# Two transformer blocks on one core: the first slot of w_in taken in plain float32, and expert 0's last unit of weights loaded beside the ring

## The chip, the cores and the metric

The kernel runs on one NeuronCore of one Trainium2 chip. It is one program on that core's engines: TensorE (PE), VectorE (DVE), ScalarE (ACT), GpSimd (POOL) and SyncE (SP), which here only issues transfers. The metric is the time of one execution on the device in microseconds; less is better.

## The reference, cut to what matters

256 tokens of width 1024 pass two blocks. The first block is a conditioned transformer layer (modulation from `c @ w_ada`, norm, attention of two kinds, an MLP with squared ReLU). The second is a mixer (a linear recurrence and a differential attention, gated) followed by 16 experts. The parts that the change touches are the first projection and the experts:

```python
sh1, sc1, g1, sh2, sc2, g2 = jnp.split(c_act @ w_ada + b_ada, 6)
h = rmsnorm(x, norm_gains[0]) * (1.0 + sc1) + sh1
proj = h @ w_in                                   # (256, 1024) @ (1024, 2304)
...
aff = softmax(h @ w_router)                       # (256, 16)
g, idx = top_k(aff.T, 32)                         # each expert takes 32 tokens
xe = h[idx]                                       # (16, 32, 1024)
hid = silu(xe @ w_gate) * (xe @ w_up)             # w_gate, w_up: (16, 1024, 2048)
ye = (hid @ w_down) * g                           # w_down: (16, 2048, 1024)
out = rms_norm(x + zeros.at[idx].add(ye))
```

Everything is float32. The experts' weights are 16 x 3 x 8 MB, 403 MB in all, read once.

## The kernel before, in words

**The prelude.** All weights ahead of the experts come in 99 slots of 1 MB ([128, 2048] float32), numbered by `g`: 8 of w_ada (`G_ADA0`), 9 of w_in (`G_WIN`), 16 of w_ada, 4 of w_out, 32 of the MLP, 14 and 8 of the second w_in (`G_MIX2`, `G_GATES2`), 4 + 4 of the last projections. SP issues them in that order into a ring of 6 slots; a load waits until the slot six places earlier has been used or split. The large products run in three passes: ACT rounds a slot to fp32r (`round_slot`, L353), DVE or POOL subtracts to get the rest (`residue_slot`, L361), the activations are handled likewise (`round_tile`, `residue_tile`), and PE multiplies rounded x rounded, rounded x rest and rest x rounded (`product`, L491 to L493). The split slots have two buffers (`wR`), so `round_slot(g)` waits until PE is done with the split slot two places earlier. Slots listed in `RAW` skip all that: `raw_channels` (L532) multiplies them in plain float32, a tile of 128 tokens at a time.

**The start.** PE multiplies the 8 slots of w_ada as they arrive (`ada`, L564), turns the rows of gains and biases into columns and the modulation row into columns (`turn`, L485). DVE and ACT write the normed and modulated hidden state `hT` (`place`, L1000 and L1591), round and split it, and then the first two slots of w_in. ACT issues 14 small transfers in `late_loads()` (L1536 to L1550) behind those two slots and ahead of the third. From w_in's fourth slot comes the attention bias: DVE writes a row, POOL stores it and reads it back in 16 transfers (L1870), copies a part, and DVE waits for the copy (`bias_copied`, ahead of L1091) before the attention.

**The experts.** An expert has 6 units of 4 MB: two of w_gate, two of w_up, two of w_down, numbered `u` from 0 to 95. They go through 5 buffers (`expert_ring`, buffer `u % 5`), the memory that the prelude's ring and split buffers leave. Units 0 to 4 are issued as the prelude frees that memory; unit `u` from 5 on waits for `pairs_used`, which PE raises twice per unit when it has multiplied a half. Units of gate and up come as one transfer, each partition reading 32 KB in a row; units of down as two transfers of 2 MB with 16 KB in a row each (`halved`), as does unit 5. PE gathers the tokens of four experts (L906), multiplies gate and up with four tiles of 32 columns side by side (L931), turns the hidden values (L485), multiplies down (L956) and scatters (L964).

## Time and profile before

| | us |
|---|---|
| median of 3 runs | 1537.79 |
| lowest and highest | 1537.52, 1540.73 |
| the profiled execution, its own time | 1543.38 |
| its span in the profile | 1541.0 |

| engine | busy us | share |
|---|---|---|
| PE, multiplying | 1134.6 | 74% |
| DVE | 404.3 | 26% |
| ACT | 317.6 | 21% |
| POOL | 54.9 | 4% |

The profile cuts the span into 40 slices of 38.5 us. The first 16 or so hold the prelude, the rest are the experts. In the chain of work that ended last 52% of the span are transfers and 41% PE. A busy PE need not be at its peak; the trace gives the clock that PE was granted, at 1.00 for 2.4 GHz and 0.50 for 1.2 GHz.

### The profile page before, as it was taken

The numbers are of one execution on the slowest core, as the hardware profiler recorded it, in microseconds if no ns is written. First come the engines' busy times: TensorE is split into PE (matmuls) and PEld (weight loads), VectorE is DVE, ScalarE is ACT, GpSimd is POOL, SyncE is SP. The second block draws the span as 40 slices with busy tenths as digits, with TensorE's granted clock in tenths as the row PEclk, the third lists the DMA queues.
The fourth block names the chain that finished last, engine by engine and source line by source line (L and its number), as shares of the span: only waits on it lengthen the run. The fifth ranks groups of instructions, "written<-read, shape, count | busy, mean of one in ns | idle before, by whom it ended". The sixth has DMA issues, their size and how long they took to land.

```text
span 1541.0 us, 17000 instructions
## 1 busy us (share of the span) xinstructions
PE 1134.6 (74%) x7468; PEld 667.3 (43%) x7468; DVE 404.3 (26%) x731; ACT 317.6 (21%) x543; POOL 54.9 (4%) x50
## 2 busy tenths in 40 slices
PE   3999999998999779965657656657656567565555
PEld 1976898987999778411113111113111113111111
DVE  2447664655758664200000000000000000000001
ACT  3346453444644544000000000000000000000001
POOL 0020000000024300000000000000000000000000
PEclk8898999999999889978778877878788868778777
DMA  9879356552753247899999999999999999999996
GB/s 366 284 279 375 109 198 191 185 189 87 222 167 110 83 164 323 344 428 430 433 427 430 433 426 432 431 426 432 431 427 433 429 429 430 430 430 429 430 432 268
DMA packets 91507, 516.43 MB, mean 335 GB/s; under 512 B 6847, under 2 KB 63658, under 8 KB 71978
## 3 DMA queue, kind: packets, MB, share of 16 engines
q1 hardware_dynamic: 86400, 508.57, 81.3%
q10 hardware_dynamic: 4106, 4.57, 0.9%
q0 software_dynamic: 928, 2.20, 0.5%
q8 instruction: 59, 0.97, 0.3%
q14 instruction: 14, 0.11, 0.0%
HBM read 514.12 MB, written 1.07 MB: 334 GB/s over the span
## 4 chain that ended last, share of the span: by engine, by line
DMA 52%; PE 41%; DVE 4%; ACT 2%; issue 1%; ACTq 0%; SPq 0%; DVEq 0%
DMA expert_ring<-in_w_up_e 19%; DMA expert_ring<-in_w_gate_e 17%; DMA expert_ring<-in_w_down_e 15%; PE PS L491 9%; PE PS L492 9%; PE PS L493 9%; PE PS L931 6%; PE PS L485 2%; DMA ring<-in_w_ada 1%; PE PS L956 1%; PE PS L564 1%; PE PS L906 1%; PE PS L532 1%; DVE wR L361 1%; PE PS L526 0%
## 5 line engine op out<-in xcount | busy, mean ns | idle before, releaser
L931 PE MATMUL PS<-expert_ring,xeT 128*32 128x512 f32 x2048 | 350.0, 847 | 239.2 <-DMA expert_ring<-in_w_up_e 121.3
L931 PEld LDWEIGHTS PS<-expert_ring,xeT 128*32 128x32 f32 x2048 | 81.4, 148 | 506.4 <-issue 238.7
L1501 DVE TENSOR_TENSOR expert_rows<-expert_rows,PS 128x512 f32<-128x512 f32 x16 | 11.0, 687 | 819.4 <-PE PS L931 819.4
L491 PE MATMUL PS<-hR,wR 128*128 128x256 f32 x648 | 187.4, 289 | 16.3 <-DVE wR L361 16.3
L956 PE MATMUL PS<-expert_ring,expert_rows 128*32 128x512 f32 x1024 | 141.0, 687 | 73.0 <-DMA expert_ring<-in_w_down_e 64.2
L353 ACT ACTIVATE wR<-ring 128x1024 fp32r<-128x1024 f32 (+2 forms) x146 | 146.3, 1051 | 217.1 <-PE PS L493 217.1
L492 PE MATMUL PS<-hR,wR 128*128 128x256 f32 x648 | 185.9, 287 | 0.0
L493 PE MATMUL PS<-hR,wR 128*128 128x256 f32 x648 | 185.7, 287 | 0.0
L361 DVE TENSOR_TENSOR wR<-ring,wR 128x1024 fp32r<-128x1024 f32 x130 | 153.2, 1221 | 106.4 <-ACT wR L353 106.3
L491 PEld LDWEIGHTS PS<-hR,wR 128*128 128x128 f32 x648 | 127.1, 196 | 18.4 <-issue 18.3
L492 PEld LDWEIGHTS PS<-hR,wR 128*128 128x128 f32 x648 | 127.2, 196 | 0.0
L493 PEld LDWEIGHTS PS<-hR,wR 128*128 128x128 f32 x648 | 126.9, 196 | 0.0
L956 PEld LDWEIGHTS PS<-expert_ring,expert_rows 128*32 128x32 f32 x1024 | 30.5, 118 | 167.0 <-DMA expert_ring<-in_w_down_e 99.6
L491 PE MATMUL PS<-wR,hR 128*128 128x256 f32 (+1 forms) x272 | 78.5, 288 | 3.1 <-DVE wR L361 1.6
L1833 ACT ACTIVATE expert_rows<-PS 128x512 f32<-128x512 f32 x16 | 9.6, 597 | 339.8 <-PE PS L931 339.8
L492 PE MATMUL PS<-wR,hR 128*128 128x256 f32 (+1 forms) x272 | 78.0, 287 | 0.0
L493 PE MATMUL PS<-wR,hR 128*128 128x256 f32 (+1 forms) x272 | 78.0, 287 | 0.0
L1838 ACT ACTIVATE selx<-PS 128x256 f32<-128x256 f32 x16 | 6.1, 383 | 342.9 <-PE PS L485 342.9
L491 PEld LDWEIGHTS PS<-wR,hR 128*128 128x128 f32 x272 | 53.5, 197 | 5.9 <-DVE hR L1436 2.3
L492 PEld LDWEIGHTS PS<-wR,hR 128*128 128x128 f32 x272 | 53.5, 197 | 0.0
L493 PEld LDWEIGHTS PS<-wR,hR 128*128 128x128 f32 x272 | 53.4, 196 | 0.0
L1840 ACT ACTIVATE expert_rows<-PS 128x512 f32<-128x512 f32 x16 | 9.6, 597 | 208.3 <-PE PS L956 208.3
(256 smaller groups left out, 1074.9 us busy)
## 6 DMA issues: line engine op xcount, KB each, us to landing
expert_ring<-in_w_gate_e SPq DMA_DIRECT2D x32, 4096.0 KB, 42.9
expert_ring<-in_w_up_e SPq DMA_DIRECT2D x32, 4096.0 KB, 43.6
expert_ring<-in_w_down_e SPq DMA_DIRECT2D x64, 2048.0 KB, 43.6
ring<-in_w SPq DMA_DIRECT2D x32, 1024.0 KB, 5.5
ring<-in_w_in SPq DMA_DIRECT2D x31, 1024.0 KB, 5.8
ring<-in_w_ada SPq DMA_DIRECT2D x24, 1024.0 KB, 9.9
ring<-in_w_out SPq DMA_DIRECT2D x8, 1024.0 KB, 8.8
arena<-bias_scratch POOLq DMA_DIRECT2D x16, 128.0 KB, 5.8
```

What stands on the lines that cost most here:

```text
L353: nc.scalar.activation(halves(g, 0)[:, piece], slot(g)[:, piece], ACT.Copy).then_inc(slot_rounded, 1)
L361: by.tensor_tensor(halves(g, 1)[:, piece], slot(g)[:, piece], halves(g, 0)[:, piece], ALU.subtract)\
L485: return nc.tensor.transpose(out_, in_, ident[0:n, 0:n])
L491: nc.tensor.matmul(o, first[0], second[0], start=start, stop=False, skip_group_check=onto)
L492: nc.tensor.matmul(o, first[0], second[1], start=False, stop=False, skip_group_check=onto)
L493: return nc.tensor.matmul(o, first[1], second[0], start=False, stop=stop, skip_group_check=onto)
L532: mm = nc.tensor.matmul(PS[:, bank, m * S + t * P:m * S + (t + 1) * P], k8(g)[:, k, m * P:(m + 1) * P], hT[:, k, t * P:(t + 1) * P], start ...
L564: mm = nc.tensor.matmul(PS[32 * j:32 * j + 32, bank, :], crep[:, k, :], slot(g)[:, 512 * j:512 * (j + 1)], start=(k == 0), stop=(k == 7), ...
L906: mm = nc.tensor.matmul(o, work[:, t, k::KD], sel[t][:, GROUP * group:GROUP * (group + 1), :] .rearrange("p e c -> p (e c)"), start=(t == ...
L931: mm = nc.tensor.matmul(PS[32 * j:32 * j + 32, kind // 2, :], xeT[:, e // GROUP % 2, k, own], w[:, 512 * j:512 * (j + 1)], start=(k == 0), ...
L956: mm = nc.tensor.matmul(PS[32 * at:32 * at + 32, 3, :], hidT[:, c, q, :], w[:, c, 512 * half:512 * (half + 1)], start=(q == 0 and c < 2), ...
L1501: V.tensor_tensor(hid[:, :], silu[:, :], PS[:, 1, :], ALU.mult).then_inc(hid_set, 1)
```

## The change

There are five edits. (1) w_in's first slot joins `RAW`: no rounding and splitting of it; PE multiplies it per token tile as soon as that tile of `hT` is placed, and ACT places both tiles before it rounds them. (2) PE gets 30 float32 products of the identity with itself (`turned_awake`) between the slots of w_ada and behind the turned modulation row, and turns the gains' rows behind the sixth w_ada slot, not behind the eighth. (3) Expert 0's last unit (`APART`, u = 5) leaves the ring and lies in four other places: 2 MB in a new tensor `ahead`, 1 MB in `ybuf`, and half a MB each in `xeT`'s second half and in `const`. The ring now takes 95 units, counted by `fill_of` and `unit_of`. (4) w_down is laid out in two pieces of rows per expert, not four, so a partition reads 32 KB in a row and a down unit is one transfer; only unit 6 and the last are still halved. For that the hidden values must come in another order, so gate's and up's moving operand is read as runs of 4 floats with 4 left out between them. (5) To make room, the scratch for POOL's transfers is set to 1024 bytes, `selx` moves into `const`, and a square's throwaway output goes to `work`.

```diff
 BUFFERS = 5
+APART = 5
-RAW = (G_MLP, G_MIX2)
+RAW = (G_WIN, G_MLP, G_MIX2)
+        ahead = sb("ahead", [P, 2 * SLOT])
-        selx = sb("selx", [P, S])
+        selx = nc.alloc_sbuf_tensor_at("selx", [P, S], F32, offset=const_at + 4 * C_DIST)
+        sixth = [ahead[:, c * D:(c + 1) * D] for c in range(4)] + [ahead_y[:, 0:D], ahead_y[:, D:2 * D], ahead_x, ahead_c]
+        def fill_of(u):
+            return u - (u > APART)
+        def unit_of(n):
+            return n + (n >= APART)
         def halved(u):
-            return u % UNITS_EACH >= 4 or u == BUFFERS
+            return u in (APART + 1, EXPERTS * UNITS_EACH - 1)
...
         def _(sp):
+            down = A["w_down_e_2"][0].rearrange("e (q p c) n -> e q p (c n)", q=2, p=P)
             for g, (dst, src) in enumerate(loads):
+                if g == G_GATES2 + 4:
+                    sp.dma_start(ahead[:, :], down[0, 1][:, 0:4 * D]).then_inc(ahead_loaded, 16)
...
-            down = A["w_down_e_2"][0].rearrange("e (q p c) n -> e q p (c n)", q=4, p=P)
             for u in range(EXPERTS * UNITS_EACH):
-                e, kind, b = u // UNITS_EACH, u % UNITS_EACH, u % BUFFERS
+                e, kind, n = u // UNITS_EACH, u % UNITS_EACH, fill_of(u)
+                b = n % BUFFERS
...
                 if u == 1:
+                    sp.wait_ge(act_split, 2 * TBRANCH + 2)
+                    sp.dma_start(ahead_y, down[0, 1][:, 4 * D:6 * D]).then_inc(ahead_loaded, 16)
                     sp.wait_ge(mixed, 2)
...
+                if u == APART:
+                    sp.wait_ge(logit16, 1)
+                    sp.dma_start(ahead_x, down[0, 1][:, 6 * D:7 * D]).then_inc(ahead_x_loaded, 16)
+                    sp.wait_ge(rank_cols, 1)
+                    sp.dma_start(ahead_c, down[0, 1][:, 7 * D:8 * D]).then_inc(ahead_c_loaded, 16)
+                    continue
+                if n >= BUFFERS:
+                    sp.wait_ge(pairs_used, 2 * unit_of(n - BUFFERS) + (1 if halved(u) else 2))
...
+            def turned_awake(times):
+                for _ in range(times):
+                    nc.tensor.matmul(PS[:, 1, 0:P], ident, ident, start=True, stop=True)
...
+                if k == 5:
+                    pe.wait_ge(rows_in, 16 * 5)
+                    pe.wait_ge(rows_in_pool, 16 * 4)
+                    turn(PS[:, 0, 0:A_ROWS], rowsA[:, :], A_ROWS)
+                    turn(PS[:, 0, A_ROWS:A_ROWS + B_ROWS], rowsB[:, :], B_ROWS).then_inc(cols_turned, 1)
+                if k >= 3:
+                    turned_awake(5 if k < 7 else 2)
             pe.wait_ge(modrow_set, 1)
             turn_mod(0, 3)
+            turned_awake(8)
+            for t in range(NT):
+                pe.wait_ge(placed[0], 2 * T1 + t + 1)
+                pe.wait_ge(placed[1], 2 * T1 + t + 1)
+                if t == 0:
+                    arrived(pe, G_WIN)
+                mm = raw_channels(G_WIN, 0, t)
+            mm.then_inc(slots_used, 1)
             pe.wait_ge(act_split, 2 * T1 + 2)
...
-                        w = expert_ring[:, FILL[u % BUFFERS], r * SLOT:(r + 1) * SLOT]
+                        w = expert_ring[:, FILL[fill_of(u) % BUFFERS], r * SLOT:(r + 1) * SLOT]\
+                            .rearrange("p (q n h c) -> p q h n c", q=2, n=P, h=2)
                         for j in range(4):
                             mm = nc.tensor.matmul(PS[32 * j:32 * j + 32, kind // 2, :], xeT[:, e // GROUP % 2, k, own],
-                                                  w[:, 512 * j:512 * (j + 1)], start=(k == 0), stop=(k == KD - 1),
+                                                  w[:, j // 2, j % 2, :, :], start=(k == 0), stop=(k == KD - 1),
...
-            for g in range(G_WIN, G_WIN + 2):
-                residue_slot(dve, V, g)
+            residue_slot(dve, V, G_WIN + 1)
...
-            place(T1, 4, hT, lambda k: fold[:, 0, k:k + 1], lambda k: shift1[:, k:k + 1])
-            for g in range(G_WIN, G_WIN + 2):
-                round_slot(act, g)
+            place(T1, 4, hT, lambda k: fold[:, 0, k:k + 1], lambda k: shift1[:, k:k + 1], split=False)
+            for t in range(NT):
+                round_tile(T1, hT, t)
+            round_slot(act, G_WIN + 1)
             late_loads()
...
-    nc = _bacc.Bacc("TRN2", target_bir_lowering=False, num_devices=1)
+    nc = _bacc.Bacc("TRN2", target_bir_lowering=False, num_devices=1, dynamic_dma_scratch_size=1024)
```

Line numbers in the changed file differ: `turn` is L511 there, `product` L517 to L519, `ada` L595, `raw_channels` L563, `turned_awake` L557, `round_slot` L359.

This is PE's program before, from the last three slots of w_ada to the first slot of w_in (`ring<-` here is w_ada, `hR,wR` the split hidden state and weights; [waits ...] are the semaphores ahead of an instruction):

```order
L564 MATMUL PS<-ring,crep 32x512 [waits loaded1]
L564 MATMUL PS<-ring,crep 32x512 x3
L485 MATMUL PS<-const,arena 128x112 [waits rows_in_pool,rows_in]
L485 MATMUL PS<-const,arena 128x69
L485 MATMUL PS<-const,arena 128x128 [waits modrow_set]
L485 MATMUL PS<-const,arena 128x128 x3
L491 MATMUL PS<-hR,wR 128x256 [waits slot_split_dve,act_split]
```

And the same place in the changed program (L557 with `const` alone are the added products):

```order
L595 MATMUL PS<-ring,crep 32x512 [waits loaded1]
L595 MATMUL PS<-ring,crep 32x512 x3
L557 MATMUL PS<-const 128x128 x2
L511 MATMUL PS<-const,arena 128x128 [waits modrow_set]
L511 MATMUL PS<-const,arena 128x128 x3
L557 MATMUL PS<-const 128x128 x8
L563 MATMUL PS<-hT,ring 128x128 [waits loaded2,placed_act,placed_dve]
L563 MATMUL PS<-hT,ring 128x128 x15
L563 MATMUL PS<-hT,ring 128x128 [waits placed_act,placed_dve]
L563 MATMUL PS<-hT,ring 128x128 x15
L517 MATMUL PS<-hR,wR 128x256 [waits slot_split_dve,act_split]
```

What PE does first behind the turned row no longer waits for a split, and the first split product is now that of w_in's second slot.

ACT's program around the small transfers before (`hT` placed and rounded per tile, then two slots rounded, then the transfers, of which the first and last are shown, then the third slot):

```order
L1600 ACTIVATE hR<-hT 128x8x128 [waits placed_act,placed_dve]
L353 ACTIVATE wR<-ring 128x1024 [waits loaded2]
L353 ACTIVATE wR<-ring 128x1024
L353 ACTIVATE wR<-ring 128x1024 [waits loaded3]
L353 ACTIVATE wR<-ring 128x1024
L1536 DMA relb<-in_rel_bias 32x16
...
L1550 DMA arena<-in_norm_gains 128x1024
L353 ACTIVATE wR<-ring 128x1024 [waits slots_used,loaded4]
```

And in the changed program:

```order
L1651 ACTIVATE hR<-hT 128x8x128 [waits placed_act,placed_dve] x2
L359 ACTIVATE wR<-ring 128x1024 [waits loaded3]
L359 ACTIVATE wR<-ring 128x1024
L1587 DMA relb<-in_rel_bias 32x16
...
L1601 DMA arena<-in_norm_gains 128x1024
L359 ACTIVATE wR<-ring 128x1024 [waits loaded4]
```

The third slot's rounding has lost its wait for PE (`slots_used`) but still stands behind the 14 transfers.

SP's program at the experts' start, before:

```order
L465 DMA expert_ring<-in_w_gate_e 128x8192 [waits normed]
L465 DMA expert_ring<-in_w_gate_e 128x8192 [waits mixed]
L465 DMA expert_ring<-in_w_up_e 128x8192 [waits slot_split_dve]
L465 DMA expert_ring<-in_w_up_e 128x8192 [waits slots_used]
L470 DMA expert_ring<-in_w_down_e 128x4096 x2
L470 DMA expert_ring<-in_w_down_e 128x4096 [waits pairs_used] x2
L465 DMA expert_ring<-in_w_gate_e 128x8192 [waits pairs_used] x2
```

And in the changed program:

```order
L491 DMA expert_ring<-in_w_gate_e 128x8192 [waits normed]
L475 DMA ybuf<-in_w_down_e 128x2048 [waits act_split]
L491 DMA expert_ring<-in_w_gate_e 128x8192 [waits mixed]
L491 DMA expert_ring<-in_w_up_e 128x8192 [waits slot_split_dve]
L491 DMA expert_ring<-in_w_up_e 128x8192 [waits slots_used]
L491 DMA expert_ring<-in_w_down_e 128x8192
L483 DMA xeT<-in_w_down_e 128x1024 [waits logit16]
L485 DMA const<-in_w_down_e 128x1024 [waits rank_cols]
L497 DMA expert_ring<-in_w_gate_e 128x4096 [waits pairs_used] x2
L491 DMA expert_ring<-in_w_gate_e 128x8192 [waits pairs_used]
```

The first transfer that waits for PE to free a buffer is now expert 1's first gate unit; expert 0's second down unit is issued in pieces ahead of it.

## Rows read from the trace of the kernel before

**Rows 1.** The page: GB/s moved in each of 40 slices of 38.5 us.

```profile
GB/s 366 284 279 375 109 198 191 185 189 87 222 167 110 83 164 323 344 428 430 433 427 430 433 426 432 431 426 432 431 427 433 429 429 430 430 430 429 430 432 268
```

**Rows 2.** Stretches: length, busy us by engine, then PE's clock, DMA share, GB/s.

```profile
40.70:46.40 5.70, 5.64 (x26) 5.67 (x27) 2.18 (x2) 0.17 (x1) 0.00 (x0) 0.50 1.07 363
...
626.00:632.00 6.00, 6.00 (x34) 5.16 (x36) 1.72 (x3) 0.00 (x0) 0.00 (x0) 0.94 0.14 60
...
651.00:1529.00 878.00, 542.11 (x3206) 153.12 (x3202) 30.29 (x64) 23.66 (x45) 0.00 (x0) 0.80 1.00 428
```

**Rows 3.** PE in order of time, experts: start us, length us, instruction, [idle before <-releaser].

```profile
695.05 1.92 PE L956 MATMUL PS<-expert_ring,expert_rows 128*32 128x512 f32 x16 [0.48 <-DMA expert_ring<-in_w_down_e]
...
704.84 3.35 PE L956 MATMUL PS<-expert_ring,expert_rows 128*32 128x512 f32 x16 [2.97 <-DMA expert_ring<-in_w_down_e]
...
714.55 5.34 PE L931 MATMUL PS<-expert_ring,xeT 128*32 128x512 f32 x32 [3.59 <-DMA expert_ring<-in_w_gate_e]
...
734.01 6.25 PE L931 MATMUL PS<-expert_ring,xeT 128*32 128x512 f32 x32 [3.72 <-DMA expert_ring<-in_w_up_e]
```

**Rows 4.** SP's transfers in order of time at the experts' start.

```profile
606.27 28.63 SPq L470 DMA_DIRECT2D expert_ring<-in_w_down_e  x4
638.00 3.76 SPq L465 DMA_DIRECT2D expert_ring<-in_w_gate_e  x2
```

**Rows 5.** PE in order of time from the ranks' transposes to the first units.

```profile
622.15 0.29 PE L485 MATMUL PS<-const,top_rows 16*128 16x16 f32 x2 [1.06 <-DVE top_rows L1464]
...
630.87 13.94 PE L931 MATMUL PS<-expert_ring,xeT 128*32 128x512 f32 x128
```

**Rows 6.** The chain that ended last: start us, us, what.

```profile
369.93 3.57 PE PS L532 x32
...
623.02 7.92 PE PS L906 x32
...
1528.57 3.26 PE PS L956 x16
```

**Rows 7.** PE in order of time at the start, and behind one later gap.

```profile
17.71 1.06 PE L564 MATMUL PS<-ring,crep 128*32 128x512 f32 x8
...
26.47 1.94 PE L564 MATMUL PS<-ring,crep 128*32 128x512 f32 x8 [1.48 <-DMA ring<-in_w_ada]
...
30.07 1.11 PE L485 MATMUL PS<-const,arena 128*128 128x128 f32 x4 [1.17 <-DVE arena L1045]
...
509.16 1.11 PE L485 MATMUL PS<-const,arena 128*128 128x128 f32 x4 [5.02 <-DVE arena L1353]
```

**Rows 8.** The clock behind that gap.

```profile
511.00:513.00 2.00, 2.00 (x11) 2.00 (x11) 1.90 (x5) 0.10 (x1) 0.00 (x0) 0.50 0.98 332
```

**Rows 9.** DVE and ACT in order of time, w_in's first three slots (ACTq: ACT issues transfers).

```profile
31.84 2.64 DVE L1000 TENSOR_SCALAR hT<-PS,fold,modcol 128x128 f32<-128x128 f32 x8
...
34.44 1.49 ACT L1591 ACTIVATE hT<-PS,modcol,fold 128x128 f32<-128x128 f32 x4
...
36.16 0.32 ACTq L1536 DMA_DIRECT2D relb<-in_rel_bias  x1
...
47.87 0.46 ACTq L1550 DMA_DIRECT2D arena<-in_norm_gains  x1
...
49.34 2.01 ACT L353 ACTIVATE wR<-ring 128x1024 fp32r<-128x1024 f32 x2 [8.47 <-PE PS L493]
...
50.50 2.36 DVE L361 TENSOR_TENSOR wR<-ring,wR 128x1024 fp32r<-128x1024 f32 x2 [7.62 <-ACT wR L353]
...
55.10 2.01 ACT L353 ACTIVATE wR<-ring 128x1024 fp32r<-128x1024 f32 x2 [3.75 <-PE PS L493]
```

**Rows 10.** POOL reads the attention bias back; DVE's first instruction behind that wait.

```profile
76.78 8.49 POOL L1870 DMA_DIRECT2D arena<-bias_scratch  x16 [4.45 <-DMA bias_scratch<-arena]
92.21 1.89 POOL L1873 COPY arena<-arena 128x2048 f32<-128x2048 f32 x1 [6.94 <-DMA arena<-bias_scratch]
...
100.16 0.16 DVE L1091 TENSOR_SCALAR sinkneg<-sinkbc 128x8 f32<-128x8 f32 x1
```

More of the change, by code:

```diff
@@ L947, in _ @@
                 pe.wait_ge(hidT_set, e + 1)
[L948 to L953 removed]
+                for q in range(2):
+                    u = UNITS_EACH * e + 4 + q
+                    w = expert_ring[:, FILL[fill_of(u) % BUFFERS], :]
+                    w = sixth if u == APART else [w[:, c * D:(c + 1) * D] for c in range(8)]
+                    for c in range(8):
+                        if u == APART:
+                            if c % 4 == 0:
+                                pe.wait_ge(ahead_loaded, 32)
+                            if c >= 6:
+                                pe.wait_ge((ahead_x_loaded, ahead_c_loaded)[c - 6], 16)
+                        elif c % 4 == 0:
+                            unit_arrived(u, c // 4)
                         for half in range(2):
                             at = 2 * half + c % 2
[L956 to L959 removed]
+                            mm = nc.tensor.matmul(PS[32 * at:32 * at + 32, 3, :], hidT[:, c % 4, 2 * q + c // 4, :],
+                                                  w[c][:, 512 * half:512 * (half + 1)], start=(q == 0 and c < 2),
+                                                  stop=(q == 1 and c >= 6), tile_position=(0, 32 * at))
+                        if c % 4 == 3:
+                            mm.then_inc(pairs_used, 1)
                 pe.wait_ge(selx_ready, e + 1)
```

48 lines of the change are left out of this document (19 added, 29 removed).

## The prediction

> **What bounds the kernel now.** I read the page's slices first. In [rows 1] the traffic is uneven in the first seventeen slices and then stands at 426 to 433 GB/s up to the last one, and the stretch from 651 to 1529 us has a DMA share of 1.00 while PE's clock is 0.80 [rows 2]. So there are two regimes. In the experts transfers set the pace: in PE's order of time each product of a unit begins when its unit has landed, with 3 to 4 us of idle PE ahead of it [rows 3], and the chain ends with the last down half, 3.26 us of PE from 1528.57 us [rows 6]. Only fewer bytes in that stream, a better rate, or an earlier start of it shorten it. The start is set by the prelude, where PE and the split pipeline set the pace, because the transfer of unit 5 waits for PE to free half of unit 0. Between the two is a hole: from 626 to 632 us only 60 GB/s are moved [rows 2], since units 3 and 4 are through and unit 5 may not start before PE, which began at 630.87 us, has done half a unit [rows 5].
>
> **Edit 3, the sixth unit.** Before, the stream behind the hole carries units 5 to 95, 91 of them; now 6 to 95, 90. Unit 6 waits for the same half of unit 0 as unit 5 did. A down unit takes the stream 704.84 - 695.05 = 9.79 us [rows 3]: two halves landed one after the other. That is the gain, if unit 5's 4 MB lie in time when nobody needs the queue. 2 MB are issued with the gates' slots, where the slices show 83 to 167 GB/s [rows 1], against 430 possible; they push the next slot's load back by 2.1/0.43 = 4.9 us, and a slot is loaded six slots ahead, two of which the split takes, so more than 20 us of cover remain. 1 MB is issued right behind unit 0, in a wait of SP for `mixed`. The last two half MB are issued at `logit16` and at the ranks' transposes, 622.15 us [rows 5], and queue behind units 3 and 4: those were issued at 606.27 us [rows 4] and end at about 606.3 + 2 x 9.75 = 625.8 us, so the last piece lands at about 625.8 + 1.05/0.43 = 628.2 us, ahead of 632.6 us, when the stream restarts (630.87 plus half of 13.94/4 us [rows 5]). SP's new waits have only unit 6's issue queued behind them, which waits longer anyway. Cost nothing, gain **9.8 us**. Were the cover gone (all 4 MB behind 632 us), the gain would be 0.
>
> **Edit 4, longer runs.** In one and the same stream three units of gate and up land in 734.01 - 704.84 = 29.17 us, 9.72 us each, and the down unit before them took 9.79 [rows 3]. The two kinds differ in the length of the run (32 against 16 KB) and the number of transfers (one against two). With both made equal I take 0.07 us for each of 30 down units (all but unit 5, counted above, and the last): **2.1 us**. Bounds: 0, and 3 us with 0.1 us each.
>
> The price of this edit is the strided moving operand of gate and up. The trace has no strided moving operand. The nearest row is the gather L906, whose stationary operand takes one float in eight: its 32 records took 7.92 us where the 32 of the raw product L532, of the same size, took 3.57 us [rows 6], a factor of 2.2. Below nothing it can't go. At 2.2 a unit at full clock takes 3.48 x 2.2 = 7.7 us in place of 3.48, still less than the 9.72 us in which the next one lands, so it is paid once: half a unit ahead of the stream's restart, 2.1 us. I take 0, being nearer to whole runs of four than to single floats, and keep 2.1 us for the range. The Trainium skill (SBUF — State Buffer, the note on SBUF cachelines) says that accesses in one 16-byte line run at full rate and each new line costs; four floats in a row use whole lines, so by that rule this read costs nothing and the gather's eightfold step does; by the rule the sum is as I give it, by the gather's factor 2.1 us worse.
>
> **Edits 1 and 2, the start.** I follow the moment at which PE starts w_in's third slot; from there each slot is PE's as before. Before, it is 55.10 us: ACT's row there was released by PE's last product of the second slot, and the third follows at once [rows 9].
> - The last w_ada slot took 1.94 us at half clock, earlier ones 1.06 us [rows 7]. With the added products (0.22 us each by L532, 16 products in 3.57 us [rows 6]) PE hardly stands still, so I let the clock stay up: the slot ends at about 28.1 us, not 28.41. The gains' rows are already turned and copied, which takes some 0.6 us out of the way to the modulation row's turn, and that takes 0.6 in place of 1.11 us [rows 7]. So the placing starts at about 30.2 us in place of 31.84 [rows 9]: 1.6 us earlier.
> - PE starts the raw product of tile 0 at 30.2 + 1.6 = 31.8 us and works 2 x 3.6 us [rows 6], to 39.1 us. Meanwhile ACT rounds both tiles and the second slot, DVE follows; by the durations of about 1.0 and 1.2 us a piece (2.01 and 2.36 us for two [rows 9]) that is done at about 39.2 us. PE does the second slot at full clock in 48 x 0.12 = 5.76 us (55.10 - 49.34 [rows 9]), to **45.0 us**.
> - The third slot's rounding no longer waits for PE, but ACT has its transfers ahead of it. They ran from 36.16 to 48.33 us, 12.2 us, starting as soon as the second tile was placed, at 34.44 + 1.49 = 35.93 us [rows 9]. Now both tiles are placed by 30.2 + 3.0 = 33.2 us; the transfers end at about 33.4 + 12.2 = 45.6 us. From ACT's start to DVE's end the split takes 50.50 + 2.36 - 49.34 = 3.5 us [rows 9], so PE gets the third slot at **49.1 us**. This is 6.0 us earlier, with a new wait of 4.1 us in it. Before, that stretch of ACT was covered by PE's slow first slot.
> - A gap of this size costs clock: behind one of 5.02 us [rows 7] the clock was 0.50 [rows 8], and at 0.50, 26 products took 5.64 us [rows 2] that take 3.1 us at full clock, 2.5 us lost. I take 2.1 us. Net **3.9 us**.
>
> Bounds for this part: nothing, if the clock is lost longer or the attention waits for something else; and 55.10 - 45.0 = 10.1 us, if the transfers do not hold ACT up.
>
> **Edit 5.** POOL's smaller scratch could slow its 16 transfers of the bias. They are issued in 8.49 us, the last lands 6.94 us later, the copy ends at 94.10 us, and DVE comes to that wait at 100.16 us [rows 10]. All of it hangs on w_in's fourth slot and moves with it, so 6.1 us of cover remain. No row of before shows POOL waiting for room. I take 0. The moved `selx` and `work` change no instruction's size: 0.
>
> **Sum**, against the profiled execution: 1543.4 - 9.8 - 2.1 - 3.9 = 1527.6 us. The median of the runs lies 5.6 us below the profiled time, so the forecast is **1522.0 us**.
>
> **Rivals.**
> - *A, ACT's transfers don't hold the third slot up* (they are shorter when fewer other transfers run, or ACT gets to the rounding between them). For it: that 12.2 us were never on the path, so nothing shows what they really need. Against it: they stand ahead in ACT's order, and 14 of them at the 0.32 to 0.46 us of the first and the last [rows 9] are still some 5.5 us. Then the start gives 10.1 us and no clock is lost: 1537.8 - 9.8 - 2.1 - 10.1 = 1515.8 us.
> - *B, the start gives nothing, the stream gives its part:* clock lost for a whole slot behind the new gap, or the strided read at 2.2, or both; 1537.8 - 11.9 = 1525.9 us, to 1528 with the 2.1 us.
> - *C, slower: POOL's transfers run one behind the other.* In before the 16 overlap: 8.49 + 6.94 = 15.4 us in all. With room for one at a time each takes its issue of 0.53 us and some 6 us to land, 16 x 6.5 = 104 us, 89 us more; less 6.1 of cover and 15.8 of gain it is 67 us slower, 1605 us. It decides when the bias comes more than 6.1 + 15.8 = 21.9 us later, which takes two or fewer in flight (16/2 x 6.5 = 52 us against 15.4). For it: the edit cuts exactly what these transfers use. Against it: no row. No run here shows it yet. Seven in flight at some 6 us each end 3 to 4 us later than now, which the 6.1 us cover.
> - *D, the sixth unit saves nothing* because its pieces collide with what needs the queue; 1537.8 - 6.0 = 1531.8 us. Against it stand the hole and the low slices.
>
> **How the numbers follow.** Forecast (1518 to 1525): 0.68. A: 0.14. B: 0.10. C: 0.04. D: 0.03; a strided read beyond 3 times, at which PE would bound the experts and the time rise above before: 0.01. The range from 1514 to 1527.5 leaves out C, D and a part of A and B. A difference of 0.2% (3 us) is about what a measurement of this kernel can tell from none. Faster: 0.68 + 0.14 + 0.10 + 0.03 = 0.95, less 0.02 for what I have not thought of: 0.93. Same 0.02, slower 0.05.
>
> **What would show it.** Right: in the stretch of the experts transfers fill everything from about 627 - 4 us on with no second hole; the number of units behind it is 90; a down unit lands in 9.72 us; the w_in stage has an idle PE of about 4 us between second and third slot, released by DVE, behind ACT's transfers, and the clock at 0.50 behind it; gate and up take 3.5 us per unit at full clock. Wrong: a wait of DVE for POOL's copy ahead of the attention; gate and up units of 7 us; the first products at 0.50 although the warmers ran; idle transfers behind 632 us because PE frees buffers too late.

## The result

The changed kernel takes 1528.65 us, the median of six runs (1526.48 to 1532.55). Beside it the kernel before took 1538.72 us (six runs, 1537.52 to 1543.81). The ratio is 0.9935, with a 95% interval from 0.9919 to 0.9951, so the change saves about 10 us (7.5 to 12.5). A second measurement gave 1528.48 us and a ratio of 0.9933 (0.9920 to 0.9947). The forecast was 1522.0 us with a range of 1514.0 to 1527.5: the direction is right, the size is not, and the time lies 1.2 us outside the range. Of 15.8 us that the sum promised, about 10 came.

The profiled execution of the changed kernel took 1527.02 us, with a span of 1524.7 us. I read it in the order of the prediction.

**The stream.** The slices of the changed kernel (GB/s, against [rows 1]) and three stretches (columns as in [rows 2]):

```profile
GB/s 366 293 282 376 136 177 194 192 192 69 221 230 119 84 193 303 371 438 428 429 435 428 434 432 429 433 430 432 429 431 432 430 435 426 434 432 426 437 428 264
```

```profile
46.00:52.00 6.00, 2.30 (x11) 2.30 (x11) 4.72 (x5) 4.38 (x5) 0.00 (x0) 0.76 1.17 332
624.00:629.00 5.00, 5.00 (x35) 3.23 (x39) 2.11 (x5) 0.00 (x0) 0.00 (x0) 1.00 0.26 106
...
646.00:1512.00 866.00, 517.61 (x3210) 154.98 (x3198) 30.28 (x64) 23.66 (x45) 0.00 (x0) 0.82 1.00 429
```

The hole ahead of the first units is still there, and behind it nothing pauses. In PE's order of time the first units, the two down units of the second expert with the up unit ahead and the gate unit behind, and the last down half, against [rows 3, 5, 6] (a float32 product shows as two records, so x32 is 16 products):

```profile
626.54 13.94 PE L976 MATMUL PS<-expert_ring,xeT 128*32 128x512 f32 x128
...
670.94 4.99 PE L976 MATMUL PS<-expert_ring,xeT 128*32 128x512 f32 x32 [6.08 <-DMA expert_ring<-in_w_up_e]
680.74 5.21 PE L1007 MATMUL PS<-expert_ring,expert_rows 128*32 128x512 f32 x32 [3.02 <-DMA expert_ring<-in_w_down_e]
690.50 5.34 PE L1007 MATMUL PS<-expert_ring,expert_rows 128*32 128x512 f32 x32 [4.55 <-DMA expert_ring<-in_w_down_e]
...
700.21 3.64 PE L976 MATMUL PS<-expert_ring,xeT 128*32 128x512 f32 x32 [1.58 <-DMA expert_ring<-in_w_gate_e]
...
1512.14 2.46 PE L1007 MATMUL PS<-expert_ring,expert_rows 128*32 128x512 f32 x16 [2.59 <-DMA expert_ring<-in_w_down_e]
1515.40 3.78 PE L1016 MATMUL PS<-expert_rows,selx 64*128 64x512 f32 x8 [0.79 <-ACT expert_rows L1892]
```

The first four units take 13.94 us, to the hundredth what they took with whole rows [rows 5]: the strided read costs nothing. A row that waited for a transfer begins when it has landed, so the two down units here took 680.74 - 670.94 = 9.80 and 690.50 - 680.74 = 9.76 us, and the gate unit behind them 9.71. Over the whole trace the first down unit of an expert takes 9.80 us and the second 9.62 (medians), 19.43 together; in the kernel before the two take 19.6 together. So the mean is 9.71, as forecast, but it comes from the second of the two. From the first unit to the last down half pass 1512.14 - 626.54 = 885.60 us, where it was 1528.57 - 630.87 = 897.70 [rows 5, 6]: 12.1 us less, forecast were 11.9. The last row is for later: the scatter L1016 takes 3.78 us.

SP's transfers, against [rows 4]:

```profile
601.92 0.43 SPq L491 DMA_DIRECT2D expert_ring<-in_w_down_e  x1
609.31 0.33 SPq L483 DMA_DIRECT2D xeT<-in_w_down_e  x1
618.14 0.33 SPq L485 DMA_DIRECT2D const<-in_w_down_e  x1
628.52 2.04 SPq L497 DMA_DIRECT2D expert_ring<-in_w_gate_e  x2
```

The last piece of the sixth unit is issued 10 us before the stream restarts and lands 9.0 us later, at 627.1 us; none of it is behind 628.5 us.

**The start.** PE (against [rows 7]), ACT and DVE ([rows 9]):

```profile
27.61 1.07 PE L595 MATMUL PS<-ring,crep 128*32 128x512 f32 x8 [0.81 <-DMA ring<-in_w_ada]
...
32.53 7.38 PE L563 MATMUL PS<-hT,ring 128*128 128x128 f32 x64 [0.52 <-DVE hT L1052]
...
49.70 0.58 PE L517 MATMUL PS<-hR,wR 128*128 128x256 f32 x1 [4.04 <-DVE wR L367]
```

```profile
33.99 0.32 ACTq L1587 DMA_DIRECT2D relb<-in_rel_bias  x1
...
36.27 3.36 ACTq L1593 DMA_DIRECT2D gain_rows<-in_norm_ffn_g  x1
...
40.16 4.50 ACTq L1597 DMA_DIRECT2D bmg<-in_b_mgate  x4
...
46.13 3.90 ACT L359 ACTIVATE wR<-ring 128x1024 fp32r<-128x1024 f32 x4 [8.52 <-issue]
...
58.51 2.01 ACT L359 ACTIVATE wR<-ring 128x1024 fp32r<-128x1024 f32 x2 [8.01 <-PE PS L519]
```

The third slot starts at 49.70 us (55.10 before, 49.1 forecast), behind 4.04 us of idle PE, because ACT issued its transfers first, from 33.99 to 46.08 us; two entries of them alone, L1593 and L1597, took 7.9 us. Behind the gap the clock is low (0.76 over 46 to 52 us), and the slot takes 58.51 - 49.70 = 8.8 us instead of the 5.76 of [rows 9]: 3.0 us lost, 2.1 forecast.

**The bias.** This is the chain of waits of the changed kernel, from the stored row to the attention (start us, us, what), and then three of DVE's instructions there:

```profile
69.48 4.28 DMA bias_scratch<-arena
74.05 3.75 POOL arena L1922 x7
77.80 8.20 issue
85.99 3.71 POOL arena L1922 x7
89.70 5.04 issue
94.74 1.06 POOL arena L1922 x2
95.80 2.69 issue
98.51 1.90 POOL arena L1925
```

```profile
96.38 0.42 DVE L1125 COPY arena<-PS 128x256 f32<-128x256 f32 x1 [9.77 <-PE PS L519]
...
100.43 0.17 DVE L1142 TENSOR_SCALAR sinkneg<-sinkbc 128x8 f32<-128x8 f32 x1 [2.53 <-POOL arena L1925]
100.64 0.96 DVE L1151 SCALAR_TENSOR_TENSOR hT<-PS,arena 128x768 f32<-128x768 f32 x1
```

In [rows 10] POOL issued the 16 reads in one go of 8.49 us, and DVE did not wait. Now they go in lots of 7, 7 and 2 with pauses of 8.20 and 5.04 us between them, the copy starts 98.51 - 74.05 = 24.5 us behind the first issue instead of 92.21 - 76.78 = 15.4, and the bias is on the path. DVE starts its first copy of the last results of w_in at 96.38 us, but gets past the wait only at 100.43 us, where it was at 100.16 us in [rows 10]. What edits 1 and 2 had gained at this place, 2.3 us (the same copy began at 98.72 us before), was waited away.

### The profile page after: what moved, and what is told of

Same layout as the page of the kernel before. It is cut to its first block, busy times and chain, and to the rows that moved or that the text cites. A ratio compares the mean times of both kernels' runs of the same rounds, so it can differ in the third digit from the quotient of the medians.

```text
span 1524.7 us, 17121 instructions
## 1 busy us (share of the span) xinstructions
PE 1114.1 (73%) x7544; PEld 674.8 (44%) x7544; DVE 401.8 (26%) x729; ACT 315.5 (21%) x541; POOL 54.9 (4%) x50
## 4 chain that ended last, share of the span: by engine, by line
DMA 52%; PE 39%; DVE 4%; issue 2%; ACT 1%; POOL 1%; ACTq 1%; SPq 0%; DVEq 0%; POOLq 0%
DMA expert_ring<-in_w_up_e 19%; DMA expert_ring<-in_w_gate_e 17%; DMA expert_ring<-in_w_down_e 15%; PE PS L517 8%; PE PS L518 8%; PE PS L519 8%; PE PS L976 5%; PE PS L1007 2%; DMA ring<-in_w_ada 2%; PE PS L511 1%; DVE wR L367 1%; PE PS L595 1%; PE PS L950 1%; PE PS L563 1%; POOL arena L1922 1%
## 5 line engine op out<-in xcount | busy, mean ns | idle before, releaser
L976 PE MATMUL PS<-expert_ring,xeT 128*32 128x512 f32 x2048 | 320.5, 784 | 234.3 <-DMA expert_ring<-in_w_up_e 126.6
L976 PEld LDWEIGHTS PS<-expert_ring,xeT 128*32 128x32 f32 x2048 | 76.3, 139 | 475.6 <-issue 217.3
L1007 PE MATMUL PS<-expert_ring,expert_rows 128*32 128x512 f32 x992 | 145.0, 739 | 90.4 <-DMA expert_ring<-in_w_down_e 88.3
L517 PE MATMUL PS<-hR,wR 128*128 128x256 f32 x632 | 183.3, 290 | 10.6 <-DVE wR L367 10.6
L359 ACT ACTIVATE wR<-ring 128x1024 fp32r<-128x1024 f32 (+2 forms) x144 | 144.3, 1051 | 216.1 <-PE PS L519 207.5
L518 PE MATMUL PS<-hR,wR 128*128 128x256 f32 x632 | 181.6, 287 | 0.0
L519 PE MATMUL PS<-hR,wR 128*128 128x256 f32 x632 | 181.5, 287 | 0.0
L517 PEld LDWEIGHTS PS<-hR,wR 128*128 128x128 f32 x632 | 124.4, 197 | 12.5 <-issue 8.2
L518 PEld LDWEIGHTS PS<-hR,wR 128*128 128x128 f32 x632 | 124.3, 197 | 0.0
L519 PEld LDWEIGHTS PS<-hR,wR 128*128 128x128 f32 x632 | 124.2, 196 | 0.0
L1007 PEld LDWEIGHTS PS<-expert_ring,expert_rows 128*32 128x32 f32 x992 | 37.0, 131 | 187.2 <-issue 106.5
L517 PE MATMUL PS<-wR,hR 128*128 128x256 f32 (+1 forms) x272 | 77.9, 286 | 3.6 <-DVE wR L367 2.1
L519 PE MATMUL PS<-wR,hR 128*128 128x256 f32 (+1 forms) x272 | 77.5, 285 | 0.0
L517 PEld LDWEIGHTS PS<-wR,hR 128*128 128x128 f32 x272 | 52.9, 194 | 5.6 <-DVE hR L1487 2.3
L519 PEld LDWEIGHTS PS<-wR,hR 128*128 128x128 f32 x272 | 53.0, 195 | 0.0
```

The source lines that it names most:

```text
L359: nc.scalar.activation(halves(g, 0)[:, piece], slot(g)[:, piece], ACT.Copy).then_inc(slot_rounded, 1)
L517: nc.tensor.matmul(o, first[0], second[0], start=start, stop=False, skip_group_check=onto)
L518: nc.tensor.matmul(o, first[0], second[1], start=False, stop=False, skip_group_check=onto)
L519: return nc.tensor.matmul(o, first[1], second[0], start=False, stop=stop, skip_group_check=onto)
L976: mm = nc.tensor.matmul(PS[32 * j:32 * j + 32, kind // 2, :], xeT[:, e // GROUP % 2, k, own], w[:, j // 2, j % 2, :, :], start=(k == 0), s ...
L1007: mm = nc.tensor.matmul(PS[32 * at:32 * at + 32, 3, :], hidT[:, c % 4, 2 * q + c // 4, :], w[c][:, 512 * half:512 * (half + 1)], start=(q ...
```

## The experiments

All ratios are to the kernel before, timed on the same chip, whose medians there were 1538.3 to 1539.6 us; 0.001 is 1.54 us. Differences in us are taken from these ratios; the quotient of the two medians can lie up to 0.001 beside them. First the two kernels themselves once more.

**The changed kernel again.**

> The changed kernel once more, beside the partial ones. Each theory expects what was measured: about 10 us below the kernel before, ratio 0.9935 within 0.0010. In its trace, DVE waits 2.5 us for POOL's copy ahead of the attention. Open is whether the 3 to 4 us that the first profile of it gained between the attention and the first unit come again: if they belong to the change, the first unit begins near 626.6 us; if they are the clock's chance, anywhere from 626 to 631 us.

1528.48 us, ratio 0.9933 (0.9920 to 0.9947). DVE waited 3.39 us for POOL's copy, the attention began at 101.06 us, and the first unit at 628.94 us, not 626.54. From the attention to the first unit it took 527.9 us, in the first profile 525.9, and in the two profiles of the kernel before 530.3 and 524.6. So the 4.4 us that the first pair of profiles shows there are not the change's.

**The kernel before again.**

> The kernel before once more, for a second profile. Its first profile was of an execution 5 us above its median and shows PE's clock at 0.57 from 137 to 149 us. If this lower clock is the execution's chance, another profile has the first unit elsewhere than at 630.9 us, while the stretch from the first unit to the last down half stays within 1 us of 897.6; ratio 1.0000 within 0.0010. If it belongs to the kernel, both come again.

Ratio 1.0004 (0.9989 to 1.0019). The profile is of an execution of 1536.68 us. Its clock from 137 to 149 us (columns as in [rows 2]):

```profile
137.00:149.00 12.00, 10.18 (x83) 9.21 (x84) 9.83 (x17) 7.52 (x9) 0.00 (x0) 1.00 1.10 348
```

It was 0.57 in the first profile. The first unit begins at 624.64 us and not at 630.87, and the stretch from there to the last down half is 898.47 us. One and the same kernel reaches the experts 6.2 us earlier or later, by the clock that PE gets in short stretches of the prelude; the stream behind varies by less than 1 us. Comparisons of two single profiles are therefore good for a stretch, not for a sum over the prelude.

**Edit 5 alone.**

```diff
-    nc = _bacc.Bacc("TRN2", target_bir_lowering=False, num_devices=1)
+    nc = _bacc.Bacc("TRN2", target_bir_lowering=False, num_devices=1, dynamic_dma_scratch_size=1024)
```

> The kernel before with one change: the scratch for POOL's transfers is 1024 bytes, nothing else. Theory (the bias is what ate the start's gain): POOL issues its 16 reads of the bias in pieces of seven, and from the first issue to the copy pass 24.5 us as in the changed kernel, not 15.4; the copy then ends 9.1 us later than before, the cover is 6.1 us, so DVE waits about 3 us for POOL's copy ahead of the attention and the time is 2.5 to 3.5 us above the kernel before (ratio 1.0016 to 1.0023). Rival (the smaller scratch costs nothing by itself, the pauses came from other traffic in the changed kernel): the 16 reads are issued without a pause, no wait of DVE, 0 us (ratio 1.0000 within 0.0008).

1543.87 us, ratio 1.0031 (1.0020 to 1.0043): 4.8 us slower. POOL and DVE in order of time:

```profile
75.50 3.75 POOL L1870 DMA_DIRECT2D arena<-bias_scratch  x7 [4.05 <-DMA bias_scratch<-arena]
87.87 3.71 POOL L1870 DMA_DIRECT2D arena<-bias_scratch  x7 [8.62 <-issue]
96.01 1.06 POOL L1870 DMA_DIRECT2D arena<-bias_scratch  x2 [4.44 <-issue]
```

```profile
101.72 0.17 DVE L1091 TENSOR_SCALAR sinkneg<-sinkbc 128x8 f32<-128x8 f32 x1 [2.35 <-POOL arena L1873]
```

The scratch alone makes the lots and the wait. The rival falls. The price (3.1 to 6.6 us by the interval) is above the 2.5 to 3.5 us that I expected, and above the 2.35 us that DVE waits.

**Other sizes: 2048 and 512 bytes.** The same line with another number.

> The kernel before with a scratch of 2048 bytes for POOL's transfers. Theory (the scratch holds a number of transfers in proportion, seven at 1024 bytes, and POOL waits until a whole lot has landed): 14 reads of the bias are issued in one go, the last two some 8 us later, the copy ends at about 97 us, still ahead of DVE at 99.5; no wait, same time as before within 0.1%. Rival (a second lot costs as much as at 1024 bytes): DVE waits, 2 to 5 us above before.

> The kernel before with a scratch of 512 bytes. Theory (three transfers in flight, a pause of about 6 to 8 us behind each lot): lots of 3, 3, 3, 3, 3 and 1, five pauses, from the first issue to the copy 50 to 55 us, DVE waits 27 to 32 us ahead of the attention and the time is that much above before, ratio 1.018 to 1.021. Rival (places come free one by one): issues in an even trickle, some 37 us to the copy, 14 us above before, ratio 1.009.

POOL at 2048 bytes, then at 512:

```profile
76.38 7.47 POOL L1870 DMA_DIRECT2D arena<-bias_scratch  x14 [4.12 <-DMA bias_scratch<-arena]
92.33 1.07 POOL L1870 DMA_DIRECT2D arena<-bias_scratch  x2 [8.48 <-issue]
```

```profile
75.35 1.72 POOL L1870 DMA_DIRECT2D arena<-bias_scratch  x3 [4.17 <-DMA bias_scratch<-arena]
84.21 1.60 POOL L1870 DMA_DIRECT2D arena<-bias_scratch  x3 [7.15 <-issue]
...
109.67 0.54 POOL L1870 DMA_DIRECT2D arena<-bias_scratch  x1 [8.76 <-issue]
```

Lots of 14 and of 3, as expected: 3, 7 and 14 transfers for 512, 1024 and 2048 bytes. At 2048 bytes the copy starts at 96.10 us and DVE does not wait: ratio 1.0001 (0.9986 to 1.0015). At 512 bytes DVE waits 15.75 us and the ratio is 1.0098 (1.0081 to 1.0115), 15 us, half of what I expected: I had taken every pause at 6 to 8 us, and three of the five were 3.0 to 3.7 us. The count of the theory stands, its price for many lots does not; the rival had about the right time with the wrong picture, an even trickle.

The landing times say when POOL goes on. Of the changed kernel's first lot, the read issued at 74.05 us, and then the two issued last, at 77.3 us (last column: median us from issue to landing):

```profile
arena<-bias_scratch POOLq DMA_DIRECT2D x1, 128.0 KB, 5.7
```

```profile
arena<-bias_scratch POOLq DMA_DIRECT2D x2, 128.0 KB, 7.4
```

The first is in at 79.8 us and the last near 84.7 us, and the next lot begins at 85.99 us. With 512 bytes it is the same in the second lot: its first read is in at 87.2 us, its last near 89.1, and the next lot begins at 89.43. POOL goes on when the whole lot is in, not when one transfer has made room for one.

**The bias read by SP.** The changed kernel, with this between the fourth and fifth load of the second lot of w_ada, and POOL's loop removed:

```diff
             for g, (dst, src) in enumerate(loads):
+                if g == G_ADA12 + 4:
+                    sp.wait_ge(bias_stored, 16)
+                    for h in range(HEADS):
+                        row = bass.AP(bias_scratch.tensor, bias_scratch.offset + h * 384, [[1, P], [1, S]])
+                        sp.dma_start(biasm[:, h, 0:S], row).then_inc(bias_in, 16)
```

> The changed kernel, but SP issues the 16 reads of the bias, between two loads of the second lot of w_ada; POOL only stores the row and copies. Theory: SP issues them in about 8 us without a pause, the copy ends at some 92 us, ahead of DVE, the attention starts at about 98 us instead of 100.6, and the time is 2 to 3 us below the changed kernel, 1525.5 to 1526.7 us, that is 12 to 13 us below the kernel before. Rival (the wait for the bias stands beside another one, or the loads that SP issues later by those 8 us hold PE up in w_ada): the gain of 2.5 us is not there or is given back, same time as the changed kernel, 10 us below before.

1525.0 us, ratio 0.9913 (0.9899 to 0.9928): 3.4 us below the changed kernel's 0.9935. SP in order of time, then DVE:

```profile
75.19 8.77 SPq L465 DMA_DIRECT2D arena<-bias_scratch  x16
84.01 24.40 SPq L471 DMA_DIRECT2D ring<-in_w_ada  x7
```

```profile
98.55 0.96 DVE L1156 SCALAR_TENSOR_TENSOR hT<-PS,arena 128x768 f32<-128x768 f32 x1 [0.26 <-PE PS L677]
```

SP issues all 16 without a pause, the copy starts at 89.60 us, DVE waits only for PE, and the loads that SP issues 9 us later hold nothing up (from the attention to the first unit pass 524.7 us). The two kernels differ in this alone, and the wait is gone. The intervals of the two ratios overlap a little, so the 3.4 us by themselves are at the edge of what can be told; the same step is measured a second time under **Both**.

**ACT's transfers behind the third slot.**

```diff
-            late_loads()
...
+                if i == 0:
+                    late_loads()
```

> The changed kernel, but ACT issues its 14 small transfers behind the third slot's rounding, not ahead of it. Theory (the third slot waits 4.0 us for ACT's transfers and then runs 2.9 us longer at half clock): PE starts the third slot at about 45.7 us at full clock and the fourth at about 52 us instead of 58.5; the end of w_in comes 5.5 to 7 us earlier, the bias with it, and the time is 5 to 7 us below the changed kernel (about 1522 to 1524 us). Rival (the gap only moves: ACT's 12 us of transfers now hold up the fourth slot's rounding by as much as they did the third's): 0 to 2 us, since the fourth slot then waits 4 us and the clock falls there.

1522.39 us, ratio 0.9894 (0.9879 to 0.9909): 6.3 us below the changed kernel. PE's first idle time behind the second slot, and DVE's last copy of w_in:

```profile
52.67 0.39 PE L517 MATMUL PS<-hR,wR 128*128 128x256 f32 x1 [0.30 <-DVE wR L367]
```

```profile
89.95 0.42 DVE L1125 COPY arena<-PS 128x256 f32<-128x256 f32 x1 [9.77 <-PE PS L519]
```

The transfers now have PE's second and third slot as cover, ACT rounds the fourth slot at 49.09 us, and of the 4 us gap 0.3 are left; the clock from 46 to 52 us is 1.00. w_in ends 6.4 us earlier. DVE still waits 2.24 us for POOL's copy.

**Both.**

> The changed kernel with both: SP issues the reads of the bias, and ACT's small transfers stand behind the third slot's rounding. Theory: both gains add, 2.5 + 6 = 8 to 9 us below the changed kernel, about 1520 us. Rival (something else sets the attention's start once both waits are gone, or the transfers move the gap to the fourth slot): no better than the better of the two alone.

> The kernel of both start edits (bias read by SP, ACT's small transfers behind the third slot's rounding) once more, as a comparison on the same chip: 20 us below before, ratio 0.9865 within 0.0014, 13.0 us from the last down half to the end.

1517.96 us, ratio 0.9865 (0.9850 to 0.9879), and again 1519.44 us, 0.9874 (0.9857 to 0.9890): 20 us below the kernel before and twice the gain of the change. The attention begins at 91.84 us. The gains add: 3.4 + 6.3 us by themselves, 10.8 together. The rival is out. Moving the bias to SP behind the other step is worth 4.4 us (0.9894 to 0.9865), so both pairs show the cost of the wait.

**Without edits 1 and 2, and these alone.** The first is the changed kernel with w_in's first slot split as before and no added products; the second the kernel before with the raw slot, the added products and ACT's new order, scratch as before. The line that goes with the difference, in the first:

```diff
-RAW = (G_WIN, G_MLP, G_MIX2)
+RAW = (G_MLP, G_MIX2)
```

> The changed kernel without edits 1 and 2: w_in's first slot split as before, no added products. It keeps the sixth unit, the longer runs and the small scratch. Theory (the stream's part is 12.1 us, the start's 2.3 us are eaten by the bias): the attention starts 3 us later than in before because the small scratch delays the bias behind a start that is not earlier, so the time is 12 - 3 to 12 - 5.6 = 6.5 to 9 us below before, ratio 0.994 to 0.996, that is 1 to 4 us above the changed kernel. Rival (edits 1 and 2 gain nothing or cost): the same time as the changed kernel or less.

> The kernel before with edits 1 and 2 alone, scratch as before. Theory (these two give 2.3 us at the end of w_in, and with the large scratch nothing eats them): 16 reads of the bias without a pause, DVE does not wait for POOL, the attention starts at about 98.3 us and the time is 2.3 to 3.9 us below before, ratio 0.9975 to 0.9985. Rival (the time behind the attention does not follow its start, another wait takes it): 0 within 0.8 us.

The first: 1533.11 us, ratio 0.9962 (0.9949 to 0.9975), 5.9 us below before and 4.5 us above the changed kernel beside it (0.9933). The second: 1536.26 us, ratio 0.9980 (0.9967 to 0.9992), 3.1 us below before; its attention begins at 98.56 us without a wait for POOL. So by the ratios edits 1 and 2 are worth 3 to 4.5 us, each figure good to about 2 us, and it is the scratch beside them that takes as much away again.

**Edit 4 alone.** PE's reads and the order of the hidden values are changed as in the diff ahead, and

```diff
-            return u % UNITS_EACH >= 4 or u == BUFFERS
+            return u in (BUFFERS, EXPERTS * UNITS_EACH - 1)
...
-            down = A["w_down_e_2"][0].rearrange("e (q p c) n -> e q p (c n)", q=4, p=P)
+            down = A["w_down_e_2"][0].rearrange("e (q p c) n -> e q p (c n)", q=2, p=P)
```

> The kernel before with edit 4 alone: down units as one transfer with 32 KB in a row, gate and up read in runs of four floats. Theory: a down unit lands in 9.72 us instead of 9.79, the strided read costs nothing, 2.1 us below before, ratio 0.9986. Rival (the length of a run has no part in it, the 0.07 us came from something else): no difference, ratio 1.0000 within 0.0008. A third way, the strided read costs at the first units: the first four take more than 13.94 us.

1536.35 us, ratio 0.9987 (0.9974 to 1.0000): by the ratio the expected 2 us, at the edge of what can be told. In the trace 896.14 us pass from the first unit to the last down half, against 898.2 on the mean of the six profiles without edits 3 and 4 (897.70 to 898.47). But then this came behind (PE; the last row is the scatter):

```profile
1526.89 2.93 PE L959 MATMUL PS<-expert_ring,expert_rows 128*32 128x512 f32 x16 [2.60 <-DMA expert_ring<-in_w_down_e]
1530.61 3.78 PE L968 MATMUL PS<-expert_rows,selx 64*128 64x512 f32 x8 [0.79 <-ACT expert_rows L1844]
```

and in the second profile of the kernel before:

```profile
1518.25 3.52 PE L956 MATMUL PS<-expert_ring,expert_rows 128*32 128x512 f32 x16 [2.96 <-DMA expert_ring<-in_w_down_e]
1523.11 1.92 PE L956 MATMUL PS<-expert_ring,expert_rows 128*32 128x512 f32 x16 [1.34 <-DMA expert_ring<-in_w_down_e]
...
1525.85 1.99 PE L964 MATMUL PS<-expert_rows,selx 64*128 64x512 f32 x8 [0.81 <-ACT expert_rows L1840]
```

The same eight records of the scatter (four products) take 1.99 us at a granted clock of 1.00 and 3.78 us at 0.50. From the last down half to the end of the span it is 11.1 us in five of the six profiles without edits 3 and 4 (12.4 in the one behind the forecast), 13.1 us here, and 12.6 to 13.6 us in all nine with the sixth unit. What is slow there is the last down half (3.53 us without edits 1 and 2), the scatter, or both in part. In the short tails a low clock is there too, but it falls on the half before the last: that one takes 3.52 us and the last 1.92 in the second profile of the kernel before, and the wait for the last transfer covers it.

**Unit 94 in two halves.** I took it that the last expert's first down unit, now in one piece, lets PE idle and then work in one lump.

```diff
-            return u in (APART + 1, EXPERTS * UNITS_EACH - 1)
+            return u in (APART + 1, EXPERTS * UNITS_EACH - 2, EXPERTS * UNITS_EACH - 1)
```

> The kernel before with edit 4, but the last expert's first down unit, u = 94, also comes in two halves as before. Theory (with unit 94 in one piece PE idles longer ahead of it, works through it in one lump, and the clock is at half speed in the scatter behind the last half): the scatter is back at 2.0 us, from the last down half to the end 11.1 us instead of 13.1, and the first unit to the end takes 907.4 us, against 909.25 with edit 4 as it was and 909.4 without it. Rival (the strided reads or the order of the products do it): 13 us behind the last half as with edit 4 alone.

> The changed kernel with unit 94 in two halves. Theory: from the last down half to the end 11.1 us instead of 12.6 to 13.1, 1.5 to 2 us below the changed kernel, 1526.8 us, ratio to the kernel before 0.9920. Rival: no difference, ratio 0.9934.

> The changed kernel with all three repairs: the bias read by SP, ACT's small transfers behind the third slot's rounding, unit 94 in two halves. Theory: another 1.9 us below the kernel with the first two, about 1516 us, ratio to before 0.985. Rival: the same as with the first two, ratio 0.9865.

In the kernel before with edit 4 the tail is back at 11.3 us (scatter 1.99 us), ratio 0.9990 (0.9977 to 1.0003), where it was 0.9987. In the changed kernel nothing came of it: ratio 0.9936 (0.9920 to 0.9953), and with the other two repairs 0.9871 (0.9854 to 0.9888) against 0.9874 beside it. There the tails are 13.6 and 12.8 us; the half before the last takes 1.92 us in both, and what is slow comes behind it:

```profile
1510.35 2.86 PE L1007 MATMUL PS<-expert_ring,expert_rows 128*32 128x512 f32 x16 [2.94 <-DMA expert_ring<-in_w_down_e]
1514.00 3.79 PE L1016 MATMUL PS<-expert_rows,selx 64*128 64x512 f32 x8 [0.79 <-ACT expert_rows L1892]
```

So my explanation fell: the half unit is not what sets the clock of the tail. That the tail is longer with the sixth unit, each time for a low clock, and mostly not without it, is what nine and six profiles show; why the low clock falls ahead of the last transfer in one group and behind it in the other, I leave open.

## Why the prediction was wrong in size

**The step that failed is edit 5.** The prediction says of the bias "so 6.1 us of cover remain" and "I take 0". Cover was indeed some 6 us, but the reads took 9.0 us longer (24.5 in place of 15.4). It is 3.4 and 4.4 us (SP's reads against POOL's) to 4.8 us (the scratch alone) in the time, where the sum had 0. The prediction had named the sign for it, a wait of DVE for POOL's copy, and that wait is in the trace. And I gave the case "enough in flight to overlap, not enough for one go" no row in my list of rivals at all: C went from nothing to 67 us.

**Edits 1 and 2, 3.9 us forecast: right as to mechanism; whether the size was right is not settled.** By the ratios they give 3.1 us alone (1.2 to 5.1) and 4.5 on top of the rest. The traces show less at the end of w_in: DVE's first copy of its last results starts at 98.0 us on the mean of the eight profiles with the first slot split (97.4 to 98.7) and at 96.1 us on that of the five with edits 1 and 2 and the old place of ACT's transfers (95.0 to 96.7), 1.9 us. One reason is the start of the sum: 55.10 us for the third slot is the latest of those eight profiles (53.80 to 55.10), by the clock from 40 to 46 us, 0.50 there and 0.70 in the second profile of the kernel before. Where the rest of the 3.1 to 4.5 us would come from, behind w_in, no profile shows. The single steps: placing began at 30.88 us (30.2), the third slot at 49.70 (49.1), idle 4.04 us (4.1), clock lost 3.0 us (2.1), and the clock at 1.00 from 28 to 46 us, so the added products did their work. Rival A fell: ACT's transfers took 12.1 us, as before, although they started earlier. That they were worth 6 to 7 us when they had a cover was in my own number for the third slot, 45.0 against 49.1 us plus the clock.

**Rivals B and D.** The measured time lies nearest to B's 1525.9 to 1528 us, and the attention of the changed kernel indeed starts no earlier than before. But B's reasons, a whole slot at low clock or the strided read at 2.2, are not what the traces show, so its number is met by luck. D fell: the sixth unit did save its part.

**Edits 3 and 4, 11.9 us: right in the stream, 12.1 us there in the first pair of profiles.** Over all profiles it is 898.2 us (six) against 885.8 us (nine, 885.46 to 886.22), 12.4 us. Edit 4 by itself is 2.0 us (896.14), or 2.6 us with unit 94 halved (895.53); 2.1 were forecast. That leaves some 10 us for the sixth unit (9.8 were forecast); no run has edit 3 alone. The strided read is free in every profile with it (13.94 us). The Trainium skill (SBUF — State Buffer, the note on SBUF cachelines) says that accesses within one 16-byte line run at full rate; by that rule a read in runs of four floats costs nothing, and these traces agree.

**What the sum did not have is the tail.** Of the stream's gain 1.6 us are given back behind the last down half (11.3 against 12.9 us on the mean of six and nine profiles), where PE's clock is low. From the first unit to the end it is 909.5 us against 898.7, 10.8 us gained.

**The account.** 10.8 us from the experts, 3.1 to 4.5 from the start, less 3.4 to 4.8 for the bias, is 9.1 to 11.9 us; measured are 10.0 and 10.3. The parts add up to the whole, within the 2 us or so to which each part is known. Of the 6.6 us between forecast and measured time, 0.9 are the start of the sum: the kernel before has 1537.79 us on three runs and 1538.72 on six. The subtraction of 5.6 us between profile and median was fair: that profile was at the high end of what this kernel does, as the second one shows.

**Open.** The wait of DVE at 1024 bytes is 2.2 to 3.4 us long and its removal is worth 3.4 to 4.8 us by the ratios. In the profiles the first unit comes at 632.5 and 633.1 us with the wait and at 624.6 to 630.9 without it (both with w_in's first slot split), which is more than the attention's own delay. PE's clock goes with the wait: over the 36 us behind the attention's start it is 0.91 to 0.95 in six of the seven profiles with the wait (1.00 in the first of the changed kernel), and 0.98 to 1.00 in all ten without. From there to the first unit pass 528.1 us on the mean with the wait and 526.7 without. That would make up the difference, but single profiles without the wait lie anywhere from 524.6 to 530.3 us, so it is a hint and not shown. And the clock of the tail, above.

## What to carry to other kernels

Before a buffer that some engine's transfers use is made smaller to win room, count how many transfers of one burst it holds: with room for the whole burst POOL issued it without a pause, and each further lot cost a full landing time, not a share of it. It costs time once this is more than the cover, as 1024 bytes did here and 2048 did not. When a wait is 6 us away from the path and an edit both takes from its cover (by making the rest earlier) and touches its duration, it needs a price of its own, with an end of the range above the cover. And small transfers issued by an engine that also computes are work of that engine: put them behind the last piece that somebody waits for.

## What the runs showed of the hardware

- POOL's scratch of 512, 1024 and 2048 bytes held 3, 7 and 14 transfers of 128 KB over 128 partitions; POOL then paused 3.0 to 8.8 us until the lot had landed.
- 16 such reads cost SP 8.77 us of issue time and POOL 8.49 us, so moving them between queues costs the same issue time; pauses came only with POOL and the small scratch.
- A moving operand in runs of four floats with four left out is read as fast as a whole row: 13.94 us for 64 float32 products (128 records) at both.
- The same kernel's experts start at 624.6 or 630.9 us, with PE's clock at 1.00 or 0.57 from 137 to 149 us.
- Four float32 products of 512 columns (eight records) took 1.99 us at a granted clock of 1.00 and 3.78 us at 0.50, and the idle time just before them was the same 0.8 us.
- Two down units in a row landed in 19.6 us with 16 KB in a row per partition and two transfers each, and in 19.43 us with 32 KB and one each; it is the second unit that got shorter (9.62 us), the first stayed at 9.80.
